# Attention values made from rows before their norm, and the norm's scratch moved to PSUM, in a decoder block on one core

## The reference

```python
h = rmsnorm(x, g_mix)                      # x * rsqrt(mean(x*x) + eps) * g_mix
proj = h @ w_in
q, k, v, f_logit, gb, gc_in, xc, g_attn, g_conv = split(proj)
attn = forgetting_attention(q, k, v, f_logit + b_f)      # 8 heads of 64
...
x = x + merged @ w_out
x = x + peer(rmsnorm(x, g_ffn), ...)       # product keys, 128 x 128 experts
x = x + sigmoid(rmsnorm(x, g_ple) @ w_ple_gate) * (p @ w_ple_proj)
return rmsnorm(x, g_final)
```

## Time and profile before

| | us |
|---|---|
| median of 3 runs | 1810.73 (1810.68 to 1811.7) |
| the profiled execution, its time | 1813.05 |
| the profiled execution, its span | 1810.3 |
| TensorE busy | 1774.5 (98%) |
| VectorE busy | 1082.2 (60%) |
| GpSimd busy | 916.2 (51%) |
| ScalarE busy | 671.6 (37%) |

### The profile page before, as it was taken

One profiled execution on the slowest core, in us unless ns is written; L12 is line 12 of the kernel. 1 busy time (PEld: TensorE's weight loads), 2 busy tenths in 40 slices (PEclk: granted clock), 3 DMA queues, 4 the chain that ended last, 5 costly groups with the idle time before them and its releaser, 6 DMA issues.

```text
span 1810.3 us, 22222 instructions
## 1 busy us (share of the span) xinstructions
PE 1774.5 (98%) x7972; PEld 1454.8 (80%) x7972; DVE 1082.2 (60%) x1929; ACT 671.6 (37%) x1031; POOL 916.2 (51%) x742
## 2 busy tenths in 40 slices
PE   6999999989999999999999999999999999999998
PEld 5777788878878788888888888888888888888886
DVE  6355521436799988862222221235888888888874
ACT  5434332333332222322222222244444444444464
POOL 6323244334336787776666666405566666664200
PEclk9999999989999999999999999999999999999999
DMA  5212122317775444444444444467999999999821
GB/s 193 88 59 71 59 93 93 116 59 312 269 242 176 148 144 145 147 146 146 146 146 144 148 146 134 144 214 249 371 374 367 373 361 382 381 364 379 318 82 47
DMA packets 155565, 360.99 MB, mean 199 GB/s; under 512 B 32064, under 2 KB 73024, under 8 KB 155328
## 3 DMA queue, kind: packets, MB, share of 16 engines
q1 hardware_dynamic: 100976, 257.47, 41.4%
q0 software_dynamic: 34816, 67.41, 10.4%
q10 hardware_dynamic: 19664, 34.70, 5.3%
HBM read 298.44 MB, written 61.01 MB: 199 GB/s over the span
## 4 chain that ended last, share of the span: by engine, by line
PE 92%; DVE 6%; ACT 1%; DMA 1%; issue 1%; ACTq 0%; DVEq 0%
PE pair L748 33%; PE pair L556 18%; PE pair L558 18%; PE pair L557 18%; PE pair L652 1%; PE pair L672 1%; PE pair L726 1%; DVE topj L1383 1%; DVE wl L1357 1%; DVE top L1381 1%; PE pair L642 0%; DVE earlier L1454 0%; DVE cand L1452 0%; DVE cand L1449 0%; PE pair L757 0%
## 5 line engine op out<-in xcount | busy, mean ns | idle before, releaser
L510 POOL DMA_INDIRECT gates<-gate_val,gate_at x384 | 415.1, 1081 | 203.8 <-issue 102.5
L1357 DVE TENSOR_TENSOR wl<-raw,wh 128x1024 fp32r<-128x1024 f32 x254 | 309.5, 1220 | 345.2 <-ACT wh L896 344.8
L896 ACT ACTIVATE wh<-raw 128x1024 fp32r<-128x1024 f32 x339 | 356.7, 1054 | 135.9 <-PE pair L558 123.2
L748 PE MATMUL pair<-hh,wh 128*128 128x512 f32 x1024 | 399.0, 390 | 3.6 <-ACT gout L1069 2.9
L748 PE MATMUL pair<-hl,wh 128*128 128x512 f32 x1024 | 398.6, 389 | 0.0
L748 PE MATMUL pair<-hh,wl 128*128 128x512 f32 x1024 | 398.5, 389 | 0.0
L493 POOL TENSOR_TENSOR wl<-raw,wh 128x1024 fp32r<-128x1024 f32 x85 | 207.2, 2443 | 332.7 <-ACT wh L896 332.7
L556 PE MATMUL pair<-wh,act_h 128*128 128x512 f32 x768 | 299.1, 389 | 0.0
L558 PE MATMUL pair<-wh,act_l 128*128 128x512 f32 x768 | 298.9, 389 | 0.0
L557 PE MATMUL pair<-wl,act_h 128*128 128x512 f32 x768 | 298.9, 389 | 0.0
L1069 ACT ACTIVATE gout<-pair 128x512 f32<-128x512 f32 x128 | 76.4, 597 | 471.9 <-PE pair L748 471.9
(11 more groups left out here) (234 smaller groups left out, 1907.1 us busy)
## 6 DMA issues: line engine op xcount, KB each, us to landing
raw<-stream SPq DMA_DIRECT2D x338, 512.0 KB, 3.6
score_dram<-gout ACTq DMA_DIRECT2D x128, 256.0 KB, 2.0
gates<-zeros SPq DMA_DIRECT2D x48, 512.0 KB, 6.0
score_in<-score_dram SPq DMA_DIRECT2D x128, 192.0 KB, 6.4
gate<-gates SPq DMA_DIRECT2D x128, 192.0 KB, 6.8
gates<-gate_val,gate_at POOLq DMA_INDIRECT x384
x<-xT SPq DMA_DIRECT2D x4, 512.0 KB, 5.2
picked<-score_dram,score_at POOLq DMA_INDIRECT x128, 5.7
```

The costliest lines, as they stand in the source:

```text
L510: nc.gpsimd.indirect_dma_start(gate_list, bass.IndirectOffsetOnAxis(ap=gate_at[:, r, k:k + 1], axis=0), gate_val[:, r, k:k + 1], None).the ...
L748: last = nc.tensor.matmul(psum[u % 2][:], w(weights, U_DENSE + u, c), halves[:, c, :], start=c == 0 and which == 0, stop=c == DC - 1 and w ...
L896: nc.scalar.activation(wh[:, n % SL, :], raw[:, n % RAW, :], ACT.Copy).then_inc(hi_done, 1)
L1357: nc.vector.tensor_tensor(wl[:, n % SL, :], raw[:, n % RAW, :], wh[:, n % SL, :].bitcast(F32), ALU.subtract).then_inc(low_own, 1)
```

## The change

- The first three matmul stages are turned round. The values are made from x times the gain, not from the normed rows: `plain_high` (ACT) and `plain_low` (DVE) split that product for each chunk into `hh` and `hl`. What is missing, the norm's factor per token, is a scale operand of the copy that takes the values out of PSUM.
- PE goes through each value unit in three sweeps of eight products: high by high, low rows by high weights, high rows by low weights, each sweep with its own wait. The norm's sums stand inside unit 1, the rows behind it.
- The normed chunks are made into the same `hh` and `hl` as PE is done with the plain ones, by waits on `unit_used`; ACT copies the values between normed chunks 5 and 6. The gate products, into bank 6 now, wait chunk by chunk.
- Squares and normed chunks of both norms go through banks 4 and 5 in place of `sq`, `hf` and slices of `gout`.
- SP issues x pair 0, weight 0, x pair 1, weight 1, x pairs 2 and 3, then the rest. The gains have a semaphore of their own. ACT loads the table for the root at its start, by a root of one element.

The diff, cut:

```diff
-            for i in range(4):
+            def load_x(i):
                 sp.dma_start(x[:, 2 * i:2 * i + 2, :], xT[2 * i:2 * i + 2].rearrange("c p t -> p c t")).then_inc(x_in[i], 16)
...
             for n in range(N_UNITS):
+                for i in {0: (0,), 1: (1,), 2: (2, 3)}.get(n, ()):
+                    load_x(i)
...
+            def values(j, part, weights, first, last_part):
+                for c in (2 * j, 2 * j + 1):
+                    if part is hl:
+                        pe.wait_ge(xl_ready, c + 1)
+                    elif first:
+                        pe.wait_ge(xh_ready, c + 1)
+                    for tt in range(TT):
+                        last = nc.tensor.matmul(psum[tt][:], part[:, c, tt * P:(tt + 1) * P],
+                                                weights[:, U_V + j, (c % 2) * CW:(c % 2 + 1) * CW],
+                                                start=first and c == 0, stop=last_part and c == DC - 1)
+                return last
             pe.wait_ge(consts2, 6)
-            norm_sums(0)
+            for j in range(4):
+                pe.wait_ge(hi_done, U_V + j + 1)
+                values(j, hh, wh, True, False)
+                if j == 1:
+                    norm_sums(0)
+                values(j, hl, wh, False, False)
+                wait_low(pe, U_V + j)
+                values(j, hh, wl, False, True).then_inc(unit_used, 1)
+                if j == 1:
+                    norm_rows(0)
             pe.wait_ge(wf_split, 1)
-            for j in range(4):
-                wait_low(pe, U_V + j)
-                for c in (2 * j, 2 * j + 1):
-                    pe.wait_ge(h_ready, c + 1)
...
             for c in range(DC):
-                last = three(psum[4][0:HEADS, :], ...
+                pe.wait_ge(h_ready, c + 1)
+                last = three(psum[6][0:HEADS, :], ...
...
-                nc.scalar.activation(sqb[:, c % 2, :], x[:, c, :], ACT.Square).then_inc(sq_ready, 1)
+                nc.scalar.activation(psum[4 + c % 2], x[:, c, :], ACT.Square).then_inc(sq_ready, 1)
...
+            def normed_high(k, c):
+                act.wait_ge(hf_ready, DC * k + c + 1)
+                nc.scalar.activation(hh[:, c, :], psum[4 + c % 2], ACT.Copy).then_inc(hh_ready, 1)
+            def plain_high(k, high_part, c):
+                nc.scalar.activation(high_part[:, c, :], x[:, c, :], ACT.Copy, scale=gain[:, k, c:c + 1]).then_inc(xh_ready, 1)
...
+            for i in range(2):
+                act.wait_ge(x_in[i], 16)
+                plain_high(0, hh, 2 * i)
+                plain_high(0, hh, 2 * i + 1)
+                if i == 0:
+                    high(0)
+                square(0, 2 * i)
+                square(0, 2 * i + 1)
+            high(1)
+            for i in range(2, 4):
+                act.wait_ge(x_in[i], 16)
+                square(0, 2 * i)
+                square(0, 2 * i + 1)
+            for c in range(4, DC):
+                plain_high(0, hh, c)
+            high(2)
+            root(0)
+            high(3)
             for c in range(DC):
+                if c == 6:
+                    act.wait_ge(unit_used, U_V + 4)
+                    for tt in range(TT):
+                        last = nc.scalar.activation(v_sb[:, tt, :], psum[tt][:], ACT.Copy, scale=factor[:, tt:tt + 1])
+                    last.then_inc(v_out, 1)
+                elif c % 2 == 0:
+                    act.wait_ge(unit_used, U_V + c // 2 + 1)
+                normed_high(0, c)
+                if c < 4:
+                    high(4 + c)
...
-                        nc.vector.scalar_tensor_tensor(out=hfb[:, c % 2, :], in0=x[:, c, :], scalar=gain[:, k, c:c + 1],
+                        nc.vector.scalar_tensor_tensor(out=psum[4 + c % 2], in0=x[:, c, :], scalar=gain[:, k, c:c + 1],
...
-                        nc.vector.tensor_tensor(hl[:, c - 1, :], hfb[:, (c - 1) % 2, :], hh[:, c - 1, :].bitcast(F32),
+                        nc.vector.tensor_tensor(hl[:, c - 1, :], psum[4 + (c - 1) % 2], hh[:, c - 1, :].bitcast(F32),
...
+            def plain_low(k, high_part, low_part, c):
+                dve.wait_ge(xh_ready, DC * k + c + 1)
+                nc.vector.scalar_tensor_tensor(out=low_part[:, c, :], in0=x[:, c, :], scalar=gain[:, k, c:c + 1],
+                                               in1=high_part[:, c, :].bitcast(F32), op0=ALU.mult,
+                                               op1=ALU.subtract).then_inc(xl_ready, 1)
+            for i in range(2):
+                plain_low(0, hh, hl, 2 * i)
+                plain_low(0, hh, hl, 2 * i + 1)
+                add_square(0, 2 * i)
+                add_square(0, 2 * i + 1)
+            for c in range(4, DC):
+                add_square(0, c)
+            for c in range(4, DC):
+                plain_low(0, hh, hl, c)
+            dve.wait_ge(const_in, 48)
             link(nc.vector.tensor_copy(wf_h[:], wf[:]))
```

More of the change, by code:

```diff
@@ L282, in peer_block_kernel @@
         x_in = [sem(f"x_in{i}") for i in range(4)]
+        gain_in = sem("gain_in")
         const_in = sem("const_in")
@@ L299, in peer_block_kernel @@
         h_ready = sem("h_ready")
+        xh_ready = sem("xh_ready")
+        xl_ready = sem("xl_ready")
         v_out = sem("v_out")
@@ L716, in _ @@
             norm_sums(1)
+            norm_rows(1)
             def score(n):
@@ L888, in _ @@
         def _(act):
-            for dst, src in ((gain, gains), (wf, w_f), (bfb, b_f), (convw, conv_w)):
+            act.dma_start(gain[:], gains).then_inc(gain_in, 16)
+            for dst, src in ((wf, w_f), (bfb, b_f), (convw, conv_w)):
                 act.dma_start(dst[:], src).then_inc(const_in, 16)
@@ L911, in root @@
                 nc.scalar.activation(factor[:], psum[6][:, 0:TT], ACT.Sqrt, bias=eps[:]).then_inc(std_ready, 1)
[L913 to L921, removed]
@@ L923, in _ @@
-            for c in range(DC):
[L924 to L929, removed]
+            def normed_high(k, c):
[3 more added lines that the diff above has]
+                nc.scalar.activation(high_part[:, c, :], x[:, c, :], ACT.Copy, scale=gain[:, k, c:c + 1]).then_inc(xh_ready, 1)
@@ new lines, in _ @@
+            act.wait_ge(consts, 6)
+            nc.scalar.activation(spare[:, 0:1], eps[:], ACT.Sqrt)
+            act.wait_ge(gain_in, 16)
+            for i in range(2):
[11 more added lines that the diff above has]
+                square(0, 2 * i + 1)
@@ L930, in _ @@
             for n in range(3):
                 next_high(U_V + n)
[L933 to L936, removed]
             next_high(U_V + 3)
             act.wait_ge(f_ready, 1)
-            nc.scalar.activation(f_row[:], psum[4][0:HEADS, :], ACT.Copy).then_inc(f_out, 1)
+            nc.scalar.activation(f_row[:], psum[6][0:HEADS, :], ACT.Copy).then_inc(f_out, 1)
@@ L1039, in _ @@
                 act.wait_ge(wo_out, c + 1)
-                square(1, sq1, c)
+                square(1, c)
                 if c < DC - 1:
                     next_high(U_OUT + c)
-            norm(1, hf1)
+            root(1)
+            for c in range(DC):
+                normed_high(1, c)
             next_high(U_OUT + DC - 1)
@@ L1215, in link, with add_square, norm @@
                 dve.wait_ge(dve_own, chain[0])
-            def add_square(k, sqb, c):
+            def add_square(k, c):
                 dve.wait_ge(sq_ready, DC * k + c + 1)
                 if c == 0:
-                    nc.vector.tensor_copy(rstd[:], sqb[:, 0, :]).then_inc(sq_used, 1)
+                    nc.vector.tensor_copy(rstd[:], psum[4]).then_inc(sq_used, 1)
                 else:
                     dve.wait_ge(sq_used, DC * k + c)
-                    nc.vector.tensor_tensor(rstd[:], rstd[:], sqb[:, c % 2, :], ALU.add).then_inc(sq_used, 1)
-            def norm(k, hfb):
+                    nc.vector.tensor_tensor(rstd[:], psum[4 + c % 2], rstd[:], ALU.add).then_inc(sq_used, 1)
+            def norm(k):
                 dve.wait_ge(std_ready, k + 1)
@@ L1232, in norm @@
                 dve.wait_ge(row_ready, k + 1)
-                if k == 3:
-                    for c in range(DC):
-                        nc.vector.scalar_tensor_tensor(out=outb[:, c, :], in0=x[:, c, :], scalar=gain[:, k, c:c + 1],
-                                                       in1=psum[7][:], op0=ALU.mult, op1=ALU.mult).then_inc(out_ready, 1)
-                    return
                 for c in range(DC + 1):
@@ L1349, in _ @@
                 if dc >= 1:
-                    add_square(1, sq1, dc - 1)
-            add_square(1, sq1, DC - 1)
-            norm(1, hf1)
+                    add_square(1, dc - 1)
+            add_square(1, DC - 1)
+            norm(1)
             def low(n):
```

25 lines of the change are left out of this document (7 added, 18 removed).

## The result

| | before | after |
|---|---|---|
| median, us | 1811.56 (6 runs, 1810.68 to 1814.82) | 1802.53 (6 runs, 1801.35 to 1804.42) |
| ratio after / before | | 0.9949, 95% interval 0.9936 to 0.9962 |
| span of the profiled execution, us | 1810.3 | 1799.6 |
| first projection's first product, us | 49.20 | 40.34 |

A forecast was written before the change was run, and what follows sets the result against it. TensorE (PE), busy 98% of the span, was taken to bound the kernel. Term 1, less idle time at its start, -8.3 us, plus term 2 (PSUM), 0, took the median from 1810.73 to 1802.4 us; range 1800.6 to 1806.8.

The forecast's parts named there:

- PE's idle time at the start: Before the first projection, PE's idle time falls from 15.28 to 6.95 us, its work unchanged: -8.3 us.
- 12 slow products: At PE's start, 12 products at the low clock take 5.26 us; if the clock rises early, six fewer, -1.2 us more.
- Sums and rows at 1.84 and 2.08 us: First norm's sums and rows on PE keep their measured durations of 1.84 and 2.08 us in the new order.
- No wait before the rows, 0.6 for the port: Before the first norm's rows, 3.7 us of products cover root and diagonal; waiting for POOL would start rows at 22.9, +0.6.
- What must keep up: Normed chunks, value copies, first projection's low part and memsets arrive before PE wants them: cost 0, at most 1 us for chunks.
- PSUM: 0 us an instruction: Scratch through PSUM costs within 0.03 us an instruction; over about 12 second-norm steps -0.4 to +0.4 us, taken as 0.
- Second norm: 0: Between the second norm's sums and first product, the change makes no difference: term 2, 0 us.
- (a): Weight 0 lands late, at 9 to 10 us, and PE starts 3 us later: -5.3, 1805.4 us; chance 0.08.
- (b): PE's clock stays at 1.2 GHz until 24.46 us, as now: -3.6, 1807.1 us; chance 0.08.
- (d): The gain is used up later, where a stage starts by a DMA's or POOL's own clock: 1810.7 us; chance 0.06.
- (e): PSUM is dear for DVE while PE accumulates; at twice the price +6.5, 1817.2 us; chance 0.03.
- (c): Squares end 2 us later, DVE steps fall beside POOL in a row, rows come 2.9 us later: 1805.3 us; chance 0.07.

The follow-up runs named there:

- The runs that delayed PE's start: Changed kernel with all four x pairs ahead of weight 0, 1807.34 us; changed kernel with the gains on the other small constants' semaphore, 1807.54 us.
- the second profile: The changed kernel run once more, unchanged, for a second look; the two profiles' times were 1801.35 and 1802.81 us.

## Why the prediction was right, point by point

- **PE's idle time at the start is the gain, and it reaches the end.** Right as to the place, and only in part as to the kind. -8.3 us was forecast, the first projection moved by 8.86 us and the medians by 9.03 (8.2 from the median the prediction started from). The runs that delayed PE's start (4.9 and 4.3 us) lengthened the time by 4.8 and 5.0. But idle time before the first projection fell by 6.4 us, from 15.28 to 7.27 + 1.61, not by 8.3; the other 2.46 are work that became shorter, 31.46 us in place of 33.92.
- **PE starts at 6.95.** It was 7.27. The two plain high parts began at 4.74, not at about 4.5, and took 1.33 us, not 1.1, as a scaled copy takes 0.71 us; so weight 0's copy began at 6.11 in place of 5.8.
- **12 slow products.** Some 9, between the two cases of the prediction, worth 0.5 us.
- **Sums and rows at 1.84 and 2.08 us.** This step failed: they stand behind 32 products now, of which the last 22 or so run fast, and take 0.80 and 0.92. That is 2.2 us which the sum did not have; 0.26 go back, as the sweeps behind them take 1.95 and 1.93. "PE's 33.92 us of work are all still there" was right as a count and wrong as a time.
- **No wait before the rows, 0.6 for the port.** This failed too: PE waited 1.61 us, and 1.32 in the second profile. The date of the rows in the port's case was right, 22.9 forecast and 22.89 measured, since split and diagonal both stood beside POOL. The wait is longer than 0.6 because PE came at 21.28 in place of 22.3. With the diagonal on ACT the wait was 0.
- **The terms together.** -8.33 + 0.32 (start) + 1.61 (wait) - 2.2 (sums and rows) + 0.26 (sweeps behind them) - 0.5 (slow products) = -8.8, against -8.86 measured. The forecast hit because errors of about 2 us stood on both sides. They are not independent: the microsecond that PE won ahead of the rows became wait, so that in dates only two errors are left, +0.6 us for the port up to the rows and -1.15 for the rows themselves. That these met within 0.6 us of the forecast is luck.
- **The signs of being right.** Two held: PE's first product near 7 us, and low parts near 0.7 us. Three did not: 12 slow products, no PE wait over 0.5 us up to the first projection, and a second norm as late as before.
- **What must keep up** did. The value copies took 2.42 us with their scale operand, not 2.07; the last low part was there at 39.3 us and PE wanted it at 39.65. The memsets ended at 46.36. Copying the values sooner is worth nothing.
- **PSUM: 0 us an instruction.** Right as a price for what the prediction priced: 756 ns against 747, 687 against 684. The copy that starts the sum of squares costs more from PSUM, 0.69 us against 0.43. As a part of the change PSUM is worth 5.4 us at the first projection, which the prediction did not say: without it its own walk (last add at 14.8, no wait before the sums) would not have held.
- **The shared port.** The sum took 0 for it and the range 0.6; it moved the rows by 0.6. Not only steps with two SBUF inputs waited but also the scaling of the unit matrix (0.28 us in its usual case, 2.19 in its longest) and, in some of the runs, the gate weight's cast (2.25 to 2.42 us, else 0.19). The Trainium skill (SBUF — State Buffer, Who interferes with whom) says this of copies, casts and scalings in a two-port mode; the trace agrees, though it does not show the mode.
- **Second norm: 0.** Neither shown nor refuted as a mean: the changed kernel was 1.5 us sooner there in its first profile and 0.2 in its second, nearly all of it by the clock.
- **Rivals.** (a), (b), (d) and (e) did not come. Of (c) the sign came, a wait before the rows, but not the cause: the squares ended 0.6 us late, not 2, and the rows came 0.6 late, not 2.9.

## What to carry to other kernels

When the engine that bounds the kernel stands idle at its start, look for work that a later factor can correct (here the norm's factor, at a copy that is made anyway) and put it ahead of the chain that makes the factor. Then look at what each of the chain's steps runs beside: here DVE steps beside a POOL subtraction took up to 2.4 us in place of 0.2 to 0.3, and a buffer in PSUM or the step on ACT took that away. Count the work that moves behind a busy stretch of PE at the duration it has at the higher clock. And where another engine sets a date, time won by PE ahead of it only lengthens PE's wait.

## What the runs showed of the hardware

- DVE and POOL: a DVE subtraction over 64 columns took 2.31 us beside POOL's in one run and 0.23 behind it in another; four scalings in a row took 4.88 us across two POOL subtractions, as one scaling got in between the two and the others only behind the second.
- ACT: a copy of 512 columns with a scale operand took 0.71 us from SBUF and 0.69 from PSUM; without one 0.63 and 0.60.
- PE: one program, two executions, and the clock fell at two different places within the same pauses of 2.2, 0.9 and 2.4 us, worth 1.3 us between sums and first product. At a pause of 2.2 us near 600 us it fell in some profiles and not in others, worth 1.6 us. A difference of 1 to 2 us in one profile of this kernel says nothing of a change.
